# Two-layer streaming-encoder trunk: index projections and top-k placed ahead of three u tiles, last q tile rotated inside the attention, y's scaling and w_out's splits placed in the last query block

## The reference, cut to what matters

```
proj = h @ w_in;  q, k, v, qi, ki, wi, u = split(proj)
q, k, qi, ki = apply_partial_rope(...)            # 8 q heads of 64, 1 k, 4 index heads of 64, 1 ki
# per block of 128 queries (4 blocks), keys up to the end of the block:
score = sum_h relu(qi_h . ki) * wi_h;  keep the top 128 keys of each query
p = softmax(q . k / 8 over the kept keys);  attn = p @ v
y = s5_ssm(u)                                     # diagonal complex state-space model, Toeplitz part plus a scan
y = gelu(y);  y = y * sigmoid(y @ glu_w + glu_b)
out = concat(rms_norm(attn), rms_norm(y)) @ w_out
```

## Time and profile before

| | us |
|---|---|
| median of 3 runs | 2129.86 |
| lowest, highest | 2129.31, 2133.25 |
| the profiled execution's own time | 2126.78 |
| its span, first to last instruction | 2125.0 |
| mean granted TensorE clock | 0.970 of full |
| PE busy / DVE / ACT / POOL | 2038.4 / 1325.0 / 694.7 / 242.3 |
| DMA moved | 264.77 MB |

### The profile page before, as it was taken

One profiled execution on the slowest core, in us unless ns is written; L12 is line 12 of the kernel. 1 busy time (PEld: TensorE's weight loads), 2 busy tenths in 40 slices (PEclk: granted clock), 3 DMA queues, 4 the chain that ended last, 5 costly groups with the idle time before them and its releaser, 6 DMA issues.

```text
span 2125.0 us, 25340 instructions
## 1 busy us (share of the span) xinstructions
PE 2038.4 (96%) x9564; PEld 1644.4 (77%) x9564; DVE 1325.0 (62%) x2099; ACT 694.7 (33%) x1058; POOL 242.3 (11%) x219
## 2 busy tenths in 40 slices
PE   6999899999889999999999999999988999999998
PEld 5788778878567788888888877788766678888887
DVE  5868855566893664643466697375779546555334
ACT  3332222341453422222342322234334433223123
POOL 0005910400000000000000195040000000000000
PEclk7899999999889999999999999999997999999999
DMA  7475646343110263533237455544322025353332
GB/s 267 128 217 155 187 134 188 101 106 94 55 40 21 92 205 117 196 93 99 87 114 223 143 169 157 157 144 117 103 61 60 1 81 175 119 179 121 108 92 77
DMA packets 395985, 264.77 MB, mean 125 GB/s; under 512 B 56560, under 2 KB 371672, under 8 KB 395864
## 3 DMA queue, kind: packets, MB, share of 16 engines
q1 hardware_dynamic: 386784, 259.89, 40.8%
q10 hardware_dynamic: 9080, 3.26, 0.7%
HBM read 254.98 MB, written 6.29 MB: 123 GB/s over the span
## 4 chain that ended last, share of the span: by engine, by line
PE 77%; DVE 12%; issue 6%; ACT 3%; DMA 1%; ACTq 0%; SPq 0%; DVEq 0%; POOL 0%; POOLq 0%
PE ps L1687 23%; PE ps L1688 22%; PE ps L1689 22%; DVE w_lo L997 2%; DVE mod_acc L1018 2%; DVE small L1374 1%; PE ps L1947 1%; ACT w_hi L689 1%; PE ps L1966 1%; DVE x L1103 1%; PE ps L2039 1%; DMA stage<-in_ffn_w 1%; DVE score L1380 1%; PE ps L1957 1%; PE ps L1895 1%
## 5 line engine op out<-in xcount | busy, mean ns | idle before, releaser
L1687 PE MATMUL ps<-h_hi,w_hi 128*128 128x512 f32 x1728 | 686.4, 397 | 17.2 <-DVE w_lo L997 13.5
L1689 PE MATMUL ps<-h_hi,w_lo 128*128 128x512 f32 x1728 | 677.0, 392 | 0.0
L1688 PE MATMUL ps<-h_lo,w_hi 128*128 128x512 f32 x1728 | 676.9, 392 | 0.0
L997 DVE TENSOR_TENSOR w_lo<-stage,w_hi 128x1024 fp32r<-128x1024 f32 (+2 forms) x322 | 394.3, 1247 | 107.6 <-ACT w_hi L689 104.7
L1687 PEld LDWEIGHTS ps<-h_hi,w_hi 128*128 128x128 f32 x1728 | 326.8, 189 | 95.8 <-DVE w_lo L997 15.5
L1689 PEld LDWEIGHTS ps<-h_hi,w_lo 128*128 128x128 f32 x1728 | 326.6, 189 | 69.8
L1688 PEld LDWEIGHTS ps<-h_lo,w_hi 128*128 128x128 f32 x1728 | 327.3, 189 | 65.3 <-issue 0.5
L689 ACT ACTIVATE w_hi<-stage 128x1024 fp32r<-128x1024 f32 (+2 forms) x322 | 319.0, 1017 | 173.5 <-PE ps L1689 165.0
L1687 PE MATMUL ps<-g_hi,w_hi 128*128 128x512 f32 x704 | 276.3, 393 | 1.0 <-DVE g_lo L1310 1.0
L1688 PE MATMUL ps<-g_lo,w_hi 128*128 128x512 f32 x704 | 274.2, 389 | 0.0
L1689 PE MATMUL ps<-g_hi,w_lo 128*128 128x512 f32 x704 | 274.1, 389 | 0.0
(11 more groups left out here) (303 smaller groups left out, 1806.9 us busy)
## 6 DMA issues: line engine op xcount, KB each, us to landing
stage<-in_ffn_w SPq DMA_DIRECT2D x210, 512.0 KB, 4.6
mod_stage<-in_mod_w SPq DMA_DIRECT2D x144, 512.0 KB, 5.5
stage<-in_ffn_w SPq DMA_DIRECT2D x64, 448.0 KB, 4.0
stage<-in_w_in SPq DMA_DIRECT2D x20, 512.0 KB, 3.9
mod_first<-in_mod_w SPq DMA_DIRECT2D x16, 512.0 KB, 9.4
stage<-in_w_out SPq DMA_DIRECT2D x16, 512.0 KB, 4.2
x_in<-in_x SPq DMA_DIRECT2D x4, 512.0 KB, 5.8
stage<-in_w_in SPq DMA_DIRECT2D x8, 256.0 KB, 3.8
```

The lines of the kernel that those rows point to most:

```text
L997: V.tensor_tensor(w_lo[:, c % RING, 0:n], stage[:, c % RING, 0:n], w_hi[:, c % RING, 0:n].bitcast(F32), ALU.subtract).then_inc(w_split_lo. ...
L1687: mm(out, hi, rhs_hi, start=first, stop=False)
L1688: mm(out, hi, rhs_lo, start=False, stop=False)
L1689: return mm(out, lo, rhs_hi, start=False, stop=last)
```

## The change

Only the mixer changes. Line numbers in the rows of the changed kernel differ (split_lo L997 is L1012, the rotation L1346 is L1362, topk_max L1374 is L1390, topk_take L1380 is L1396, the mask L1404 is L1423, the exponential L877 is L891, gelu L908 is L922, logits L1947 is L1965, turn L1957 is L1975, values L1966 is L1984).

1. Tile order: tile 1 u, 2 and 3 qi, 4 v and wi, 5 to 7 the other three u, 8 to 11 q. qi is held in the room of u's last two parts until rotated. Index products start at t = 6 instead of 8; states and y move later. SP's stores and fetches of u and y follow.
2. Top-k of block 1: 13 of its 16 rounds run before the attention instead of 8, the last three in heads 0 to 2. Blocks 2 and 3 keep their heads.
3. The scan's eight multiplications of 256 elements become four of 512 (291 counted DVE steps become 275).
4. The last q rotation (swap and three DVE operations) moves into heads 3 and 4; the splits of the last two GLU chunks move to heads 0 to 2; gelu and high part of y's last tiles move to heads 0 to 4.
5. The GLU groups move from heads 4..11 to 7..14, and with them tanh, gate, squares, root and broadcast. y's scaling moves from heads 20, 21 to 25, 26, its splits from 21..23 to 26..28. w_out's splits on ACT move from heads 6, 8, 11, 13 to 19, 23, 25, 27.

```diff
-ROPE_BANKS = ((2, 3), (6, 7), (None, 3), (None, 2), (None, 3), (None, 2), (None, 3), (None, 2))
-ROPE_TILE = (0, 0, 5, 6, 8, 9, 10, 11)
-ROPE_SLOT = {3: (0, 1), 6: (2,), 7: (3,), 9: (4,), 10: (5,), 11: (6,)}
-T_U, T_V = (1, 2, 3, 4), 7
-STATES_AT = {4: 0, 5: 1, 6: 2, 8: 3}
-Y_AT = {5: 0, 6: 1, 7: 2, 9: 3}
+ROPE_BANKS = ((2, 3), (6, 7), (None, 3), (None, 2), (None, 3), (None, 2), (None, 3), (None, 7))
+ROPE_TILE = (0, 0, 2, 3, 8, 9, 10, 11)
+ROPE_SLOT = {3: (0, 1), 4: (2,), 5: (3,), 9: (4,), 10: (5,), 11: (6,)}
+T_U, T_QI, T_V = (1, 5, 6, 7), (2, 3), 4
+STATES_AT = {4: 0, 7: 1, 9: 2, 10: 3}
+Y_AT = {6: 0, 9: 1, 10: 2, 11: 3}
-GELU_AT = {10: (0, 1), 11: (2,)}
-S5_LO_AT = {0: 0, 1: 1, 2: 2, 3: 3}
-GLU_AT = {4 + 2 * n + j: (n, j) for n in range(ST) for j in range(2)}
...
-ROOT_AT, BCAST_AT = 16, 17
-SSM_AT = {20: (0, 1), 21: (2, 3)}
+GELU_FIRST, GELU_LAST = 2, 4
+GELU_HI_AT = {0: (0, 1), 1: (2,), 4: (3,)}
+S5_LO_AT = {1: (0,), 2: (1,), 3: (2,), 5: (3,)}
+LAST_SWAP, LAST_ROPE = 3, 4
+GLU_AT = {7 + 2 * n + j: (n, j) for n in range(ST) for j in range(2)}
...
+ROOT_AT, BCAST_AT = 22, 23
+SSM_AT = {25: (0, 1), 26: (2, 3)}
-INDEX_FROM = 8
+INDEX_FROM = 6
-TOPK_WITH = [(1, 2)] * HEADS + [(2, 3)] * HEADS + [(3,)] * HEADS + [()] * HEADS
-OUT_SPLIT_AT = {6: 16, 8: 17, 11: 18, 13: 19}
+TOPK_SOON = {9: 1, 10: 1, 11: 5}
+TOPK_BEHIND = {6: 2, 8: 2}
+TOPK_WITH = [(1, 2)] * 3 + [(2,)] * 5 + [(2, 3)] * HEADS + [(3,)] * HEADS + [()] * HEADS
+OUT_SPLIT_AT = {0: 14, 1: 15, 19: 16, 23: 17, 25: 18, 27: 19}
...
@@ the scan, on DVE
-                    step.mark(V.tensor_tensor(X[0], E[0], S[0], ALU.mult))
-                    re = step.mark(V.tensor_tensor(M[0], E[1], S[1], ALU.mult))
-                    step.mark(V.tensor_tensor(X[1], E[0], S[1], ALU.mult))
-                    im = step.mark(V.tensor_tensor(M[1], E[1], S[0], ALU.mult))
+                    both = [v.unsqueeze(1).broadcast_to((P, 2, GI, J)) for v in E]
+                    step.mark(V.tensor_tensor(xr, both[0], S, ALU.mult))
+                    im = step.mark(V.tensor_tensor(s5_m, both[1], S, ALU.mult))
...
@@ ACT, in the attention's loop
                     p_exps(e)
+                    if e == GELU_LAST:
+                        gelu(3)
+                    for m in GELU_HI_AT.get(e, ()):
+                        gelu_high(m)
...
@@ DVE, the loop over t
+                    for _ in range(TOPK_SOON.get(t, 0)):
+                        topk_max(1)
+                        topk_take(1)
...
-                rope(7)
-                for n in range(2):
-                    split_lo(l, m0 + 12 + n + AHEAD)
```

More of the change, by code:

```diff
@@ L120 @@
         PREP[4 * m + i + 1] = (m, i)
-DVE_STEPS, POOL_STEPS = 291, 86
+DVE_STEPS, POOL_STEPS = 275, 86
 SMALL = 72
@@ L310, in trunk @@
         pt = qi_t
+        qi_raw = [u_t[:, 3 - i].rearrange("p s j -> p (s j)") for i in range(2)]
         att = ki_t[:].rearrange("p (h d) -> p h d", d=HD)
@@ L543, in mix_src @@
                 if m in T_U:
-                    return tiles(w_in, layer, 0, KT, COL_U + (m - T_U[0]) * P)
-                if m < T_V:
-                    return tiles(w_in, layer, 0, KT, COL_QI + (m - 5) * P)
+                    return tiles(w_in, layer, 0, KT, COL_U + T_U.index(m) * P)
+                if m in T_QI:
+                    return tiles(w_in, layer, 0, KT, COL_QI + T_QI.index(m) * P)
                 if m < 12:
@@ L919, in mixer_act @@
                         split_hi(l, m0 + t + AHEAD)
+                    if t == 11:
+                        for m in range(GELU_FIRST):
+                            gelu(m)
                     z_tile(t)
-                    if t == T_V:
+                    if t == T_V + 1:
                         v_copy()
@@ L927, in mixer_act @@
                             index_relu((t - INDEX_FROM) * IDX_HEADS + n)
-                    for m in GELU_AT.get(t, ()):
-                        gelu(m)
-                for n in range(2):
-                    split_hi(l, m0 + 12 + n + AHEAD)
                 act.wait_ge(*h_done.at(l, 2 * KT - 1))
-                gelu(3)
-                for m in range(ST):
-                    gelu_high(m)
+                gelu(2)
                 for e in range(NA):
@@ L1438, in s5_scan @@
                     dve.wait_ge(*rot_done.at(l, 0))
-                    S = [ps[:, 6, z * GI * J:(z + 1) * GI * J].rearrange("p (i j) -> p i j", i=GI) for z in range(2)]
+                    S = ps[:, 6, :].rearrange("p (z i j) -> p z i j", z=2, i=GI)
                     E = [rot[:, z, m] for z in range(2)]
@@ L1502, in mixer_dve @@
                             index_acc((t - INDEX_FROM) * IDX_HEADS + n)
-                            if t > INDEX_FROM:
+                            if t == 8:
                                 (topk_max, topk_take)[n % 2](1)
                         topk_start(t - INDEX_FROM + 1)
-                rope(7)
-                for n in range(2):
-                    split_lo(l, m0 + 12 + n + AHEAD)
+                        for _ in range(TOPK_BEHIND.get(t, 0)):
+                            topk_max(1)
+                            topk_take(1)
+                    if t in STATES_AT:
+                        s5_scan(STATES_AT[t])
                 for e in range(NA):
@@ L1524, in mixer_dve @@
                         topk_take(blocks[1])
-                    if blocks and h == HEADS - 1:
-                        topk_end(blocks[0])
-                    if e in S5_LO_AT:
-                        s5_lo(S5_LO_AT[e])
+                    for m in S5_LO_AT.get(e, ()):
+                        s5_lo(m)
+                    if e == LAST_ROPE:
+                        rope(7)
                     if e in GATE_AT:
@@ L1670, in _ @@
                 power(l, 1)
-                att_power(0)
+                for b in range(2):
+                    att_power(b)
                 power(l, 2)
-                for b in range(1, QB):
+                for b in range(2, QB):
                     att_power(b)
@@ L2077, in mixer_pe @@
                         logits(e + 1)
+                    if e == LAST_SWAP:
+                        swap(7, 11, None, 0)
                     if h == 5 and b:
```

109 lines of the change are left out of this document (57 added, 52 removed).

## The result

The changed kernel takes **2146.68 us** (median of 6 runs, 2140.7 to 2153.71); the kernel before, in the same comparison, 2130.49. The ratio is **1.0075, 95% interval 1.0044 to 1.0107: slower**, by some 16 us (0.75%), where 2123.9 was forecast with a range of 2107 to 2135. The profiled execution took 2144.21 (span 2142.3, mean granted clock 0.961) against 2126.78 (2125.0, 0.970), so there are 17.4 us to explain.

The account below looks back on a forecast made before the run. DVE was taken to bound PE before about head 16, then PE at half clock until the rise; -3.3 + 0.3 = -3.0 us a layer, -6.0 for two, took 2126.78 to 2120.8, plus 3.1 for the median: 2123.9, range 2107 to 2135.

Parts of the forecast that it names:

- Step 1: Projections to head 0, layer 0: first mask at about 561.0 against 562.64, -1.6 us, PE idle some 6 us before.
- Step 2: Heads 0 to 7, mask to mask: 19.0 us against 20.95, -1.95, with two table loads in head 4.
- Step 3: Heads 8 to 15: 26.8 us against 28.2, -1.4, putting head 16's mask at 606.8 instead of 611.77.
- Step 4: Heads 16 to 23: half clock from about 607 to 631, rising with head 21's transposition; gain at head 24 3.3 us.
- rival 2: Clock stays low through head 23, head 24 starts at 643.6; +3.3 us a layer, 2136.5 us; chance 0.14.
- Step 5: Heads 24 to 31: 3.2 us a head; moved splits and scaling on ACT and DVE add 0.3 us (0 to 1.5).
- The sum: Whole kernel: -3.3 + 0.3 = -3.0 us a layer, -6.0 for two, giving a median of 2123.9 us.
- Rival 1: Clock doesn't fall in heads 16 to 23: -11.6 us a layer, 2107 us, or 2115 in one layer only; chance 0.22.
- Rivals 3, 4 and 5: Rise in head 22 to 23, 2130 (0.15); table switch or head 4 chain, 2129; rounds no cheaper, 2128 (together 0.12).

Follow-up runs that it names:

- e8: The kernel before with one extra unused gelu behind head 4's exponential, which brings two more table loads; 2130.02 us, ratio 0.9988.
- e11: The changed kernel with GLU groups, tanh, gate, squares and sums two heads earlier, root and broadcast in heads 18 and 19; 2137.17 us, ratio 1.0054.
- e12: The changed kernel with GLU groups in heads 5 to 12, root and broadcast unmoved, three unneeded dense matmuls a head from 13; 2120.37 us, ratio 0.9983.
- e1: The changed kernel with three unneeded dense matmuls a head in heads 15 to 21 too (otherwise only from 22); 2122.48 us, ratio 0.9974.
- e5: e1 with unneeded dense matmuls also ahead of head 0's turn (18) and in heads 1 to 6 (3 each); 2122.34 us, ratio 0.9961.
- e2: The changed kernel with only root and broadcast of y's norm moved from heads 22 and 23 to 19 and 20; 2141.54 us, ratio 1.0070.

## Why the prediction was wrong

The forecast had the steps up to head 8 right and priced the clock wrong after it. Step by step, for layer 0:

- **Step 1, first mask.** Forecast 561.0 and -1.6 us; measured 561.69, net -1.5. The fourth scan took 6.71 us instead of 6.5 (546.05 to 552.76), then split, five rounds at 1.21, rotation and max as summed. PE stood 5.5 us ahead of head 0's turn, as named. Right.
- **Step 2, heads 0 to 7.** Forecast 19.0; measured 19.5 (561.69 to 581.21), in layer 1 also 19.5. The table switch cost nothing (e8). Right within 0.5; -3.0 instead of -3.55 so far.
- **Step 3, heads 8 to 15.** Forecast 26.8, measured 29.1 (layer 1 27.4). The working put one GLU group, head 7's, at half the clock. The rise came only at 589.7, so head 8's ran low as well: from its first matmul to the turn, 585.46 to 588.19, 2.73 us for six matmuls (head 7's, 580.92 to 583.65, took the same), against 1.49 at the full clock (605.28, the first of head 14's six, to 606.77). The gain fell to 2.1 instead of 5.0 at head 16. Layer 1, where the clock rose 4.6 us after head 8's mask (1622.8 to 1627.4) and not 8.5, is 1.7 us shorter. The step failed in its size, by the length of the first low stretch: 27.3 us, when it had been 13.7. With the GLU starting in head 7 instead of 4, the matmuls that had ended it came three heads later. That is in the prediction's own words ("the rise comes when the first GLU groups run") and was not carried through. The runs bear it out in part: in the seven kernels with the GLU from head 7 and no padding in the first heads the stretch lasts 23.9 to 30.7 us, in e11 and e12 with it from head 5 17.1 to 23.9, before 13.7. It is not the whole, as the same order gave both ends: in e1 the stretch ended 2.9 us after head 8's mask in layer 0 and heads 8 to 15 took 26.8 us, just the forecast; in layer 1 8.5 us after, and they took 29.1.
- **Step 4, heads 16 to 23: the step that failed.** "If the rise comes with that transposition in head 21, at about 631": it came at 644.3, 13 us later. This is rival 2's mechanism, with its point of decision (a rise later than about 639) met in both layers; it had a chance of 0.14. The prediction took the clock to rise with four small matmuls (head 21's transposition, 631.14); they ran at half clock and changed nothing. The fall was at 613.6, not 607, and per-head costs were as worked out (3.58 us for 3.6). Rival 2 too was priced too low, 2136.5 against 2146.68, mostly by the next point: with its 3.9 us a layer it comes to 2144.3.
- **A row read for the wrong head.** The prediction let head 24 start at 641.62. Those logits are head 26's: logits run one head ahead of the step, and mask 24, at 638.80, came before them. So before was already 3.9 us further on than assumed (the logits before those, head 25's, start at 637.75), and of the forecast gain of 3.3 us nothing would have been left, even with the rise at 631. Nor is the mask the right mark at head 24: PE made head 24's logits in before at 633.50 and DVE came to them 5.3 us later. Told by PE, from head 16's logits to head 24's: before 25.5 us, changed 30.6, e1 23.0; from head 24's to the last: 24.6, 27.2, 24.9.
- **Step 5, heads 24 to 31.** Forecast +0.3. From mask to mask it looks like +5.5 (26.2 against 20.7), but 20.7 starts with DVE late. By PE's logits it is +2.6 in layer 0, and with the clock held +0.3 (e1: 24.9 against 24.6). So y's scaling and the splits cost what was forecast, and the rest is the low clock that lasts into head 24 (638.96 to 644.3). That separation comes from e1; that it is the same in both layers there (24.9) supports it.
- **The sum.** Net from head 16's logits on: PE had them at 607.98 before and 608.37 after, -0.2 net; then +5.1 and +2.6 give +7.5 (rounded) at the end of layer 0's attention (the last logits 658.11 and 666.13: 8.0, less 0.58). Layer 1, with the feed-forward blocks between, adds 9.2 to make 17.2 at its last logits. The forecast was -3.0 a layer.

Rival 1 (no fall) is what e1, e5 and e12 made by padding; they reach a ratio of 0.996 to 0.998, some 4 to 8 us (e12's interval includes no change), and not the 23 us that the rival promised, since it counted 11.6 us a layer from the misread 641.62 and nothing for padding. Rivals 3, 4 and 5 did not happen: the rise came at the very end of head 23's step, behind the broadcast; the table loads cost nothing; the first mask came as summed.

Shown: the loss is time at half the clock in the heads with small matmuls (e1, e12 against the changed kernel; in e1 the moved tail costs 0.3 us a layer; e8 excludes the tables). Not settled: what decides, with the same instructions, that the clock rises after 17 us in one layer and after 48 in the other (e2, e11), why padding held it in heads 15 to 21 in e1 and left 44.4 us low in the first heads of e5's profiled execution, and why before itself falls to the changed kernel's clock in 9 of 78 executions.

## What to carry to other kernels

Where PE is both busy and slow, look for the granted clock before looking for waits, and price each head at both clocks; moving the last dense group three heads later moved the fall from 600.5 to 613.6 and the rise from 621.0 to 644.3. One profile is one draw: look at the mean clock of all executions before reading a difference of half a per cent out of two traces. Padding with unused dense matmuls can pay (21 of them a layer turned a loss of 0.75% into a gain of 0.3%), but one matmul a head did nothing, and nor did three in the order of before, where DVE makes PE stand between them. And before a row serves as a milestone, count which iteration it belongs to, and take the same engine's milestone in both kernels: a mask that came late because DVE was behind hides what PE has already done.
